# Dense networks of a two-block model: the lower right quarter of a pair's Strassen-Winograd product kept in the idle half of its PSUM bank

## The reference, cut to what matters

```
def rmsnorm(x, g):
    xf = x.astype(jnp.float32)
    y = xf * lax.rsqrt(jnp.mean(xf * xf, axis=-1, keepdims=True) + EPS)
    return (y * g.astype(jnp.float32)).astype(x.dtype)

def swiglu(x, wg, wu, wd):
    return (jax.nn.silu(x @ wg) * (x @ wu)) @ wd

x = x + 0.5 * swiglu(rmsnorm(x, ffn1_norm[l]), ffn1_wg[l], ffn1_wu[l], ffn1_wd[l])
...
x = x + 0.5 * swiglu(rmsnorm(x, ffn2_norm[l]), ffn2_wg[l], ffn2_wu[l], ffn2_wd[l])
```

## Time and profile before

| | |
|---|---|
| median of 3 runs | 3033.0 us (3029.68 to 3035.7) |
| profiled execution, its time | 3030.19 us |
| profiled execution, its span | 3028.4 us |
| PE busy | 2851.9 us (94%) |
| DVE busy | 2042.4 us (67%) |
| POOL busy | 1685.0 us (56%) |
| ACT busy | 1145.1 us (38%) |
| mean granted TensorE clock | 0.981 |

### The profile page before, as it was taken

One profiled execution on the slowest core, in us unless ns is written; L12 is line 12 of the kernel. 1 busy time (PEld: TensorE's weight loads), 2 busy tenths in 40 slices (PEclk: granted clock), 3 DMA queues, 4 the chain that ended last, 5 costly groups with the idle time before them and its releaser, 6 DMA issues.

```text
span 3028.4 us, 47936 instructions
## 1 busy us (share of the span) xinstructions
PE 2851.9 (94%) x19208; PEld 2305.2 (76%) x19208; DVE 2042.4 (67%) x2752; ACT 1145.1 (38%) x2098; POOL 1685.0 (56%) x969
## 2 busy tenths in 40 slices
PE   7999999999999999999999999999998687999988
PEld 6999867668999989998666788998796675555443
DVE  8888775758889889997767589987546764112112
ACT  5333332545333353334235443334245841111111
POOL 6999744446988779784644488885443640000000
PEclk9999999999999999999999999999999888999999
DMA  4322312002232322323300032323230005999997
GB/s 155 115 95 96 128 63 105 2 2 110 93 119 91 119 84 88 113 93 116 114 36 1 29 126 84 115 95 137 84 126 1 22 38 212 422 424 423 422 424 329
DMA packets 51769, 412.44 MB, mean 136 GB/s; under 512 B 5728, under 2 KB 5984, under 8 KB 24416
## 3 DMA queue, kind: packets, MB, share of 16 engines
q1 hardware_dynamic: 51408, 408.03, 34.5%
q0 software_dynamic: 144, 1.38, 0.1%
HBM read 407.29 MB, written 2.10 MB: 135 GB/s over the span
## 4 chain that ended last, share of the span: by engine, by line
PE 73%; DVE 11%; DMA 6%; issue 4%; ACT 3%; POOL 2%; SPq 0%; DVEq 0%; ACTq 0%; POOLq 0%
PE banks L1917 8%; PE banks L1918 8%; PE banks L1919 8%; PE banks L2217 6%; PE banks L1846 6%; PE banks L1715 5%; PE banks L1934 5%; PE banks L1935 5%; PE banks L1936 5%; DMA experts<-moe_w 4%; PE banks L2228 3%; PE banks L1794 3%; PE banks L1984 2%; DMA ring<-ffn_w 2%; PE banks L2012 2%
## 5 line engine op out<-in xcount | busy, mean ns | idle before, releaser
L931 POOL TENSOR_TENSOR ring_lo<-ring,w_hi 128x1024 fp32r<-128x1024 f32 x252 | 700.0, 2791 | 149.3 <-ACT w_hi L1088 96.0
L1088 ACT ACTIVATE w_hi<-ring 128x1024 fp32r<-128x1024 f32 x256 | 270.7, 1058 | 439.5 <-PE banks L1919 430.9
L1934 PE MATMUL banks<-ffn_hidden,down_hi 128*128 128x512 f32 x704 | 275.8, 392 | 8.4 <-DVE x L2600 8.4
L1935 PE MATMUL banks<-ffn_hidden,down_hi 128*128 128x512 f32 x704 | 275.5, 391 | 0.0
L1936 PE MATMUL banks<-ffn_hidden,down_lo 128*128 128x512 f32 x704 | 275.1, 391 | 0.0
L1917 PE MATMUL banks<-t_lo,w_hi 128*128 128x256 f32 x960 | 271.9, 283 | 1.1 <-POOL ring_lo L931 1.1
L2600 DVE SCALAR_TENSOR_TENSOR x<-banks,x 128x512 f32<-128x512 f32 x352 | 230.4, 684 | 60.2 <-PE banks L1936 58.6
L1918 PE MATMUL banks<-t_hi,w_hi 128*128 128x256 f32 x960 | 269.5, 281 | 0.0
L1919 PE MATMUL banks<-t_hi,ring_lo 128*128 128x256 f32 x800 | 225.4, 282 | 0.0
L2217 PE MATMUL banks<-experts,mix 128*64 128x256 f32 x1520 | 188.7, 389 | 15.1 <-DMA experts<-moe_w 15.1
L1917 PE MATMUL banks<-upper_lo,w_hi 128*128 128x256 f32 x640 | 183.6, 287 | 19.5 <-ACT ffn_more L1171 8.7
(11 more groups left out here) (448 smaller groups left out, 8224.2 us busy)
## 6 DMA issues: line engine op xcount, KB each, us to landing
experts<-moe_w SPq DMA_DIRECT2D x47, 2048.0 KB, 17.1
ring<-ffn_w SPq DMA_DIRECT2D x43, 2048.0 KB, 7.5
experts<-moe_w SPq DMA_DIRECT2D x48, 1024.0 KB, 16.6
ring<-mix_w SPq DMA_DIRECT2D x24, 1536.0 KB, 6.4
ring<-second_w SPq DMA_DIRECT2D x16, 1536.0 KB, 6.3
ffn_more<-ffn_w SPq DMA_DIRECT2D x44, 512.0 KB, 3.8
mix<-ffn_w SPq DMA_DIRECT2D x44, 512.0 KB, 7.8
expert_table<-moe_w SPq DMA_DIRECT2D x16, 1024.0 KB, 13.9
```

What stands on the lines that cost most here:

```text
L931: pool.tensor_tensor(operand_lo(G, i), operand(G, i), operand_hi(G, i).bitcast(F32), ALU.subtract).then_inc(w_split, 1)
L1088: act.activation(operand_hi(G, i), operand(G, i), ACT.Copy).then_inc(w_high, 1)
L1934: mm(bank[4 + q % 4], w_hi, g[:, f, 1], start=f == 0, stop=False)
L1935: mm(bank[4 + q % 4], w_hi, g[:, f, 0], start=False, stop=False)
```

## The change

The two quarters `C22[a]` no longer lie in SBUF but in columns 256 to 511 of PSUM bank 2 + a, beside the quarter that product 6 is still adding to. With that a bank holds the whole block of 512 columns as soon as the lower left quarter is finished, and `second_gate` and `second_hidden` multiply it by rms with one instruction of 512 columns instead of two of 256. Nothing else is changed; `ffn_more` columns 1536 to 2047 stay unused.

```
-    V15, C22 = two_halves(ffn_more[:, 1024:1536]), two_halves(ffn_more[:, 1536:2048])
+    V15, C22 = two_halves(ffn_more[:, 1024:1536]), [bank[2 + a][:, HALF:T] for a in range(2)]
...
-            V.tensor_tensor(C22[:, a], bank[2 + a][:, 0:HALF], V15[:, a], ALU.add).then_inc(corner_added, 1)
+            V.tensor_tensor(C22[a], bank[2 + a][:, 0:HALF], V15[:, a], ALU.add).then_inc(corner_added, 1)
...
             step(V.tensor_tensor(bank[2][:, 0:HALF], bank[2][:, 0:HALF], V1[G % 2][:, 0], ALU.add))
-            V.tensor_tensor(GATES[1][:, HALF:T], C22[:, 0], rms[:, HALF:T], ALU.mult)
-            V.tensor_tensor(GATES[1][:, 0:HALF], bank[2][:, 0:HALF], rms[:, 0:HALF], ALU.mult).then_inc(gate_scaled, 1)
+            V.tensor_tensor(GATES[1], bank[2], rms, ALU.mult).then_inc(gate_scaled, 1)
...
                 step(V.tensor_tensor(bank[3][:, 0:HALF], bank[3][:, 0:HALF], V1[G % 2][:, 1], ALU.add))
-                V.tensor_tensor(bank[3][:, HALF:T], C22[:, 1], rms[:, HALF:T], ALU.mult)
-                step(V.tensor_tensor(bank[3][:, 0:HALF], bank[3][:, 0:HALF], rms[:, 0:HALF], ALU.mult))
+                step(V.tensor_tensor(bank[3], bank[3], rms, ALU.mult))
```

## The result

| | before | changed |
|---|---|---|
| median (10 runs each) | 3033.95 us (3028.1 to 3038.2) | 3045.54 us (3039.65 to 3053.17) |
| profiled execution: time, span | 3030.19, 3028.4 us | 3053.17, 3051.0 us |

The ratio is 1.0037, with an interval of 1.0026 to 1.0048: the change makes the kernel slower by 11.6 us. I had forecast 3031 us and gave 7% to a loss of this size. The profiled execution of the changed kernel is the slowest of its ten, so it shows the loss larger than the median does: its span is 22.6 us longer. About 16 us of that lie within the dense networks and 5 us between the third and the fourth, where the edit changes nothing; I account only for what lies in the networks' pairs.

A forecast was written before the change was run, and what follows sets the result against it. PE, busy 94% of the span, was taken as the bound; 0 from steady pairs, -0.6 and -1.6 us from POOL make -2.2 us, so 3031 us on the 3033.0 median, range 3024 to 3038.

The forecast's parts named there:

- what DVE saves: 40 non-opening pairs: four multiplies of 172.1 us give way to forms of 55.6 us, saving 116.5 us, 2.9 in a pair.
- a wait for silu: In front of L2590 in most pairs: DVE waits about 2.7 us for ACT's silu, some 90 us in all.
- hidden values come at +7.4: In a steady pair, hidden values come at about +7.4 us instead of +7.83; PE needs them at +9.9, so nothing is gained.
- the first sum stays with the DMA and the period at 30.90 us: L2494 still starts at +8.79 us, its wait for raw weights 0.4 us longer; the pair's period stays 30.90 us.
- in the steady pairs freed DVE time doesn't reach PE: Steady pairs: the 2.9 us saved turn into waits for silu and a DMA, contributing 0 to the time.
- The first rival: Freed DVE time reaches PE in the dense networks' stretches, removing at most its 9.6 us idle: 3023 us; chance 0.11.
- The fall of DVE's busy time by about 116 us: Expected in the changed profile: DVE busy time falls by about 116 us, with nothing of it in the time.
- What may move at all: POOL: Where POOL works back to back, it runs 0.4 us earlier in a pair without L2578 and L2589: -2.2 us in sum.
- -0.6 us (product waits for POOL): PE's waits for POOL's low parts of weights, 2.2 us in 4 places: three shrink by 0.2 us, bounds 0 to 2.2.
- -1.6 us (sums that end 0.4 us earlier): L2494 and the adds PE waits for end 0.4 us earlier in four of six places, with POOL ahead: 1.6 us.
- a sign of being wrong: PE's waits for L2598, the adds, changing by more than 3 us in sum would show the prediction wrong.
- The slower rival: L2494 in about 12 POOL-saturated pairs falls behind another POOL instruction; 1.2 us in six gives 7 us, 3040; chance 0.09.

The follow-up runs named there:

- experiment 1: Changed kernel, but the second pair of each network keeps the old form (C22 in SBUF, two multiplies each): ratio 1.0000, 3034.36 us.
- experiment 2: Kernel before, with the new form in the second pair of each network alone: ratio 1.0043, 3045.14 us.
- experiment 4: Changed kernel; POOL waits once for its own last instruction in each network's second pair, two instructions before L2494: ratio 1.0003, 3035.18 us.
- experiment 8: Changed kernel with POOL's wait for itself in second pairs, and DVE's adds 0 and 1 ahead of the last sum: ratio 0.9971, 3025.34 us.
- experiment 10: Changed kernel, POOL's wait for itself in second pairs placed earlier, behind the first half of the down weights: ratio 1.0004, 3035.54 us.
- experiment 12: Changed kernel, adds 0 and 1 ahead of the last sum, POOL's wait for itself in second, third and fourth pairs: ratio 0.9977, 3027.15 us.

## Why the prediction was wrong

Right were, with their sizes: what DVE saves (the forms at 0.69 and 0.70 us, forecast 691 and 699 ns); that it turns into a wait for silu (97.5 us, forecast some 90); that hidden values come at +7.4; that the first sum stays with the DMA and the period at 30.90 us; and that in the steady pairs freed DVE time doesn't reach PE. The first rival, a gain of up to 9.6 us, is refuted by the same rows. The fall of DVE's busy time by about 116 us comes out as 94.7 over the whole span (2042.4 to 1947.7), since the three long sums alone add about 24 us of busy time that is waiting; the stretches, where it is 99.8, don't hold quite the same work in the slower kernel.

The step that failed is the last one, "What may move at all: POOL". It had two terms, -0.6 us (product waits for POOL) and -1.6 us (sums that end 0.4 us earlier). The first held and was too small: these waits fell from 2.2 to 0.6 us. The second has the wrong sign. It took the time for which L2578 and L2589 hold up POOL as a cost alone and forecast that PE waits less for the adds; PE waits 8.9 us more for them (17.3 against 8.4), over the 3 us that I had named as a sign of being wrong. With POOL undisturbed the sums of the second pairs end 1.7, 2.6 and 2.7 us later in three of the networks and 0.3 us earlier in the fourth, the only one that did what the term says.

One reading of the prediction is off as well: an undisturbed L2494 takes 1.22 us in the kernel before, not about 1.05. Nothing in the sum hangs on it.

The slower rival had the right place, the start of L2494 in the pairs with a saturated POOL, and the wrong mechanism, so it was priced too low. It let DVE wait "up to 2.4 us more", that is for one POOL instruction at most, because every row of before showed DVE served at the next boundary. The runs show waits through up to four instructions more, with 9 to 10 us for the sum. Its count was off too: it wanted six of twelve pairs at 1.2 us. It was three of four second pairs, at 3.3, 4.2 and 5.3 us of period in the profiled execution, part of which is the clock's lower level behind PE's stall. In the median of all executions the change costs 11.6 us, and by experiments 1 and 2 that comes from these four pairs, as far as their intervals can tell. I wrote that twelve pairs at the full price "can't be reached"; the bound for a single pair was the error. What the rival did describe shows in the first network of the profiled execution, where two first sums of 3.32 and 3.40 us (before: 1.30 and 2.77) go with periods longer by 1.1 and 2.4 us. In the medians of the changed kernel with long sums prevented (1.0003 and 0.9995) nothing of that is left.

The Trainium skill's rule, "SBUF — State Buffer", section "Who interferes with whom", says that the two exclude each other for a whole instruction and that the order of issue decides who is blocked. The first half agrees: L2494 ended at 795.35, 1.1 us behind the last POOL instruction that went ahead of it. The second half is not what these traces show: L2494 stood waiting at 785.19 and four POOL instructions that came later went first.

What stays open is why POOL's run locks DVE out. The experiments show that a pause of POOL of 0.08 us, or a DVE instruction of 256 columns, resets it, that a run up to 15 us and 6 instructions was harmless, and that from 18 us and 7 instructions on a long sum is frequent and not certain (2 of 3 at 18 to 19 us, all in third pairs). Between 15 and 18 us there is no case. Neither the place within POOL's instruction at which DVE comes nor the recorded length of POOL's instructions tells the cases apart. The runs don't look inside, and the cause of this stays open.

## What to carry to other kernels

Ask of every instruction that a change removes not only what it costs but whom it interrupts. Where two engines exclude each other and one of them works without a pause, the other's short waits can be what keeps its later ones short: give the busy engine a pause of its own (a wait for its own last instruction, 0.08 us here) before the place where the other must not be late. And put what the bottleneck engine waits for ahead of work that only has to be done by and by; that order of adds was worth 0.3%; the change cost 0.4% as it stands, and with POOL's pause and that order it gained nothing over the order alone.

## What the runs showed of the hardware that was not expected

- A DVE instruction with two SBUF inputs can wait through several POOL instructions in a row: up to 10.2 us for one that takes 1.2 us, in 15 of 16 cases until POOL stopped by itself. This happened only behind 18 us or more (7 instructions or more) of POOL work without a pause and without a DVE instruction of that kind wider than 8 columns, in 14 of 20 second pairs and 2 of 3 third ones.
- A wait of POOL for its own last instruction leaves a pause of 0.08 us and prevents it (0 of 4 second pairs in each of experiments 4, 8, 10 and 12), even when it lies 8.7 to 9.9 us back. The first network's small instructions leave the same pause by themselves.
- A two-input DVE instruction of 8 columns in between doesn't prevent it (3 of 4), one of 256 columns does (0 of 4).
- After an idle time of PE of 3.65 us its granted clock fell to the lower level for a while (a mean of 0.66 over 5 us); at that level matmuls of 512 columns start every 0.43 us instead of 0.23.
